# First norm, transposes and value projection in one block by row tiles, and the bias pieces prepared in six parts in the merge stage

## What is computed

```python
xn = rms_norm(h, attn_norm_w[layer])
proj = xn @ w_in[layer]
q_a, k_a, v_a, q_b, k_b, v_b, g_a, g_b = jnp.split(proj, in_split_points(), axis=-1)
...
merged = (jax.nn.sigmoid(g_a) * (y_a @ w_proj_swa[layer])
          + jax.nn.sigmoid(g_b) * (y_b @ w_proj_sb[layer]))
h = h + merged @ w_out[layer]
...
gu = x_blk @ w_gate_up[e] + b_gate_up[e]
u = jnp.clip(gu[:, D_FF:], -SWIGLU_LIMIT, SWIGLU_LIMIT)
act = (u + 1.0) * (g * jax.nn.sigmoid(SWIGLU_ALPHA * g))
return act @ w_down[e] + b_down[e]
```

## Time and profile before

| | |
|---|---|
| median of 3 runs | 2304.51 us (2301.51 to 2306.93) |
| the profiled execution | 2303.3 us, its span 2301.6 us |
| PE busy | 2193.7 us, 95% of the span |
| DVE, ACT, POOL busy | 1595.3, 1325.4, 575.9 us |
| mean granted TensorE clock | 0.979 of full speed |

### The profile page before, as it was taken

One profiled execution on the slowest core, in us unless ns is written; L12 is line 12 of the kernel. 1 busy time (PEld: TensorE's weight loads), 2 busy tenths in 40 slices (PEclk: granted clock), 3 DMA queues, 4 the chain that ended last, 5 costly groups with the idle time before them and its releaser, 6 DMA issues.

```text
span 2301.6 us, 38892 instructions
## 1 busy us (share of the span) xinstructions
PE 2193.7 (95%) x13820; PEld 1693.4 (74%) x13821; DVE 1595.3 (69%) x1572; ACT 1325.4 (58%) x1484; POOL 575.9 (25%) x501
## 2 busy tenths in 40 slices
PE   5999999999979996999999999999999999999997
PEld 5877767677767784777777777787887777777775
DVE  4055767676545335887887887797997778777777
ACT  4156575766444113666666665675776556555665
POOL 3621111111012002132533422232332122212222
PEclk8999999999989997999999999999999999999999
DMA  5011212122165325998998998898998889888883
GB/s 167 24 37 37 81 34 61 32 63 61 53 206 183 125 83 211 385 333 281 346 336 295 345 337 284 304 399 273 402 369 304 289 295 338 277 289 288 306 316 113
DMA packets 266324, 515.66 MB, mean 224 GB/s; under 512 B 33125, under 2 KB 76848, under 8 KB 266156
## 3 DMA queue, kind: packets, MB, share of 16 engines
q1 hardware_dynamic: 239948, 471.38, 57.0%
q0 software_dynamic: 17088, 39.14, 7.2%
q10 hardware_dynamic: 9216, 4.20, 0.6%
HBM read 475.30 MB, written 43.50 MB: 225 GB/s over the span
## 4 chain that ended last, share of the span: by engine, by line
PE 58%; DVE 1%; issue 1%; ACT 1%; DMA 0%; POOL 0%; POOLq 0%; ACTq 0%; DVEq 0%
PE ex_gu L2062 30%; PE ex_yp L2110 15%; PE ex_rest L2084 6%; PE ex_rest L2127 3%; PE ex_gu L2053 1%; PE ex_gu L2020 1%; PE ex_tr L2028 1%; PE ex_gu L2028 1%; PE ex_yp L2099 1%; DVE ex_wlo L1938 0%; PE ex_rest L2078 0%; ACT ex_whi L1682 0%; DMA ex_xg<-xn_s,ex_idx 0%; PE ex_gu L2036 0%; PE ex_tr L2020 0%
## 5 line engine op out<-in xcount | busy, mean ns | idle before, releaser
L1938 DVE TENSOR_TENSOR ex_wlo<-ex_raw,ex_whi 128x2048 fp32r<-128x2048 f32 x387 | 876.6, 2291 | 216.3 <-ACT ex_whi L1682 216.2
L1682 ACT ACTIVATE ex_whi<-ex_raw 128x2048 fp32r<-128x2048 f32 x387 | 735.4, 1925 | 220.8 <-PE ex_gu L2062 151.9
L2062 PE MATMUL ex_gu<-ex_whi,ex_xhi 128*128 128x512 f32 x1024 | 290.3, 405 | 1.0 <-DVE ex_xlo L1979 1.0
L2062 PE MATMUL ex_gu<-ex_whi,ex_xlo 128*128 128x512 f32 x1024 | 275.3, 391 | 0.0
L2062 PE MATMUL ex_gu<-ex_wlo,ex_xhi 128*128 128x512 f32 x1024 | 273.9, 389 | 0.0
L2062 PEld LDWEIGHTS ex_gu<-ex_whi,ex_xhi 128*128 128x128 f32 x1024 | 191.5, 188 | 52.3 <-issue 7.4
L2062 PEld LDWEIGHTS ex_gu<-ex_whi,ex_xlo 128*128 128x128 f32 x1024 | 192.8, 188 | 41.6
L2062 PEld LDWEIGHTS ex_gu<-ex_wlo,ex_xhi 128*128 128x128 f32 x1024 | 192.5, 188 | 40.6
L57 PE MATMUL at_job<-xnT_hi,at_whi 128*128 128x512 f32 x416 | 178.7, 430 | 2.1 <-ACT at_rs L566 2.1
L716 POOL TENSOR_TENSOR at_wlo<-at_raw,at_whi 128x1024 fp32r<-128x1024 f32 x29 | 71.7, 2473 | 427.3 <-ACT at_whi L531 427.3
L59 PE MATMUL at_job<-xnT_hi,at_wlo 128*128 128x512 f32 x416 | 164.5, 395 | 0.0
(11 more groups left out here) (309 smaller groups left out, 3662.1 us busy)
## 6 DMA issues: line engine op xcount, KB each, us to landing
ex_raw<-in_w_gate_up_dram SPq DMA_DIRECT2D x512, 512.0 KB, 7.2
ex_raw<-in_w_down_dram SPq DMA_DIRECT2D x256, 512.0 KB, 6.9
at_raw<-in_w_in_dram SPq DMA_DIRECT2D x25, 512.0 KB
gT<-at_gst SPq DMA_DIRECT2D x32, 256.0 KB, 2.4
mg_g<-gT SPq DMA_DIRECT2D x32, 256.0 KB, 3.0
n_x<-in_x_dram SPq DMA_DIRECT2D x8, 512.0 KB, 8.2
...
```

Source lines behind the costliest of these rows:

```text
L1682: nc.scalar.activation(w_hi[:, i % RING, :], raw[:, i % SLABS, :], ACT.Copy).then_inc(hi_d, 1)
L1938: nc.vector.tensor_tensor(w_lo[:, slot, :], raw[:, i % SLABS, :], w_hi[:, slot, :].bitcast(F32), ALU.subtract).then_inc(lo_d, 1)
L2062: mm = nc.tensor.matmul(gu[:, half, h, :], x[:, k, :], w[:, kk, h, :], start=k == 0 and n == 0, stop=k == KD - 1 and n == 2)
```

## The change

1. The norm and the value projection become one block, `norm_and_values`. PE turns tiles 0 and 1, and then takes in turn the value products of tile t and the transposes of tile t+2. ACT and DVE are written out in the same rhythm: squares and scales three tiles ahead, high and low parts two tiles ahead. The pairs of banks for the products are two instead of four.
2. SP issues the value weights behind row tiles 0 and 1 instead of behind all eight; the other six tiles and attention's first weights follow.
3. The bias pieces are prepared in the merge stage, in six parts of 512 columns (four of gate and up, two of down), with one buffer for the rows and two for the pieces. POOL does a part behind its split for the next tile, in tiles 0 to 5; SP stores a part and loads the next behind the gates of tiles 1 to 6. The loop over tiles on SP and POOL is unrolled for it.

```diff
+def norm_and_values(nc, x, attn_norm_w, w_in, ident, nhalf, raw, raw_in, xnT_hi, xnT_lo, va, vb, x_in):
+
...
+        raw_v = sb("raw_v", [P, KD, VW])
+        w_hi = sb("pv_whi", [P, KD, VW], F32R)
+        w_lo = sb("pv_wlo", [P, KD, VW], F32R)
         tr = ctx.enter_context(nc.psum_tensor("n1_tr", [P, 4, HALF], F32))
-        w_in_ = sem("n1_w_in")
...
             @block.sync
             def _(sp):
-                for t in range(NT):
+                def load_rows(t):
                     sp.dma_start(xin[:, t, :], x_t[t]).then_inc(x_in[t], 16)
-                load_value_weights(sp, w_in, raw_v, rawv_in)
+
+                load_rows(0)
+                sp.dma_start(wB[:, :], attn_norm_w[0:1, :].to_broadcast([P, D])).then_inc(w_in_, 16)
+                load_rows(1)
+                sp.dma_start(raw_v[:, :, 0:P], w_v[:, :, VA:VA + P]).then_inc(rawv_in, 16)
+                sp.dma_start(raw_v[:, :, P:VW], w_v[:, :, VB:VB + HALF]).then_inc(rawv_in, 16)
+                for t in range(2, NT):
+                    load_rows(t)
+                load_first_tiles(sp, w_in, raw, raw_in)
 
             @block.scalar
             def _(act):
-                for t in range(NT):
+                def square(t):
                     act.wait_ge(x_in[t], 16)
-                    if t:
-                        act.wait_ge(sq_done, t)
+                    after(act, sq_done, t)
                     nc.scalar.activation(junk[:, :], xin[:, t, :], ACT.Square,
                                          accum_out=ssq[:, t:t + 1]).then_inc(sq_done, 1)
+
+                def high(t):
+                    for g in range(2):
+                        m = 2 * t + g
+                        act.wait_ge(tr_done, m + 1)
+                        nc.scalar.activation(xnT_hi[:, 4 * g:4 * g + 4, t * P:(t + 1) * P],
+                                             tr[:, m % 4, :].rearrange("p (k c) -> p k c", k=4),
+                                             ACT.Copy).then_inc(hi_done, 1)
+
+                def split_hi(k):
+                    if k == 0:
+                        act.wait_ge(rawv_in, 32)
+                    nc.scalar.activation(w_hi[:, k, :], raw_v[:, k, :], ACT.Copy).then_inc(whi_d, 1)
+
+                def take_first(t):
+                    bank = acc[:, 2 * (t % 2), :]
+                    act.wait_ge(mm_done, 2 * t + 1)
+                    nc.scalar.activation(va[:, t, :], bank[:, 0:P], ACT.Copy)
+                    nc.scalar.activation(vb[:, t, 0:VH - P], bank[:, P:VH], ACT.Copy).then_inc(ev_first, 1)
+
+                square(0)
+                square(1)
+                high(0)
+                high(1)
+                for k in range(KD):
+                    split_hi(k)
+                square(2)
+                for t in range(NT):
+                    if t + 3 < NT:
+                        square(t + 3)
+                    take_first(t)
+                    if t + 2 < NT:
+                        high(t + 2)
 
...
+                def split_lo(k):
+                    dve.wait_ge(whi_d, k + 1)
+                    nc.vector.tensor_tensor(w_lo[:, k, :], raw_v[:, k, :], w_hi[:, k, :].bitcast(F32),
+                                            ALU.subtract).then_inc(wlo_d, 1)
+
+                def take_second(t):
+                    dve.wait_ge(mm_done, 2 * t + 2)
+                    nc.vector.tensor_copy(vb[:, t, VH - P:HALF], acc[:, 2 * (t % 2) + 1, 0:VH]).then_inc(ev_second, 1)
+
+                scale_tile(0)
+                scale_tile(1)
+                low(0)
+                low(1)
+                for k in range(KD):
+                    split_lo(k)
+                scale_tile(2)
+                for t in range(NT):
+                    if t + 3 < NT:
+                        scale_tile(t + 3)
+                    take_second(t)
+                    if t + 2 < NT:
+                        low(t + 2)
+
             @block.tensor
             def _(pe):
...
+                def turn(t):
                     pe.wait_ge(xs_done, t + 1)
+                    for g in range(2):
+                        m = 2 * t + g
+                        after(pe, lo_done, m - 3)
+                        for k in range(4):
+                            last = nc.tensor.transpose(tr[:, m % 4, k * P:(k + 1) * P],
+                                                       xs[:, t % 2, (4 * g + k) * P:(4 * g + k + 1) * P], ident[:, :])
+                        last.then_inc(tr_done, 1)
+
+                def values(t):
+                    pe.wait_ge(lo_done, 2 * t + 2)
                     for h in range(2):
-                        if t >= 4:
-                            pe.wait_ge(ev_second if h else ev_first, t - 3)
+                        if t >= 2:
+                            pe.wait_ge(ev_second if h else ev_first, t - 1)
                         for k in range(KD):
                             if t == 0 and h == 0:
-                                pe.wait_ge(lo_done, k + 1)
-                            last = split3(nc, acc[:, 2 * (t % 4) + h, 0:VH],
+                                pe.wait_ge(wlo_d, k + 1)
+                            last = split3(nc, acc[:, 2 * (t % 2) + h, 0:VH],
                                           xnT_hi[:, k, t * P:(t + 1) * P], xnT_lo[:, k, t * P:(t + 1) * P],
                                           w_hi[:, k, h * VH:(h + 1) * VH], w_lo[:, k, h * VH:(h + 1) * VH],
                                           k == 0, k == KD - 1)
                         last.then_inc(mm_done, 1)
+
+                turn(0)
+                turn(1)
+                for t in range(NT):
+                    values(t)
+                    if t + 2 < NT:
+                        turn(t + 2)
 
 
...
+BIAS_PARTS = 6
+UP_PARTS = (2, 3)
+
+
+def bias_steps(c):
+
+    return 6 + 7 * c + sum(u < c for u in UP_PARTS)
+
+
+def merge(nc, w_proj_swa, w_proj_sb, ident, gT, y_s, mT_hi, mT_lo, w_out, raw_o, raw_o_in, y_in, ring, wo_hi, wo_lo,
+          b_gate_up, b_down, bp_s):
 
...
+        brow = sb("mg_brow", [3 * NE, HALF])
+        pieces = sb("mg_pieces", [P, 2, HALF], BF16)
+        pick = sb("mg_pick", [P, NE], BF16)
+        b_in, b_d, b_out = sem("mg_b_in"), sem("mg_b_d"), sem("mg_b_out")
...
-                over_tiles(sp, body)
+                def load_bias(c):
+                    src = b_gate_up[0, :, c * HALF:(c + 1) * HALF] if c < 4 else b_down[0, :, (c - 4) * HALF:(c - 3) * HALF]
+                    for q in range(3):
+                        sp.dma_start(brow[q * NE:(q + 1) * NE, :], src).then_inc(b_in, 16)
+
+                def store_bias(c):
+                    sp.wait_ge(b_d, bias_steps(c + 1))
+                    sp.dma_start(bp_s[:, c * HALF:(c + 1) * HALF], pieces[:, c % 2, :]).then_inc(b_out, 16)
+
+                load_bias(0)
+                for m in range(KD):
+                    body(m, m % 2, m < KD - 1)
+                    if m in range(1, BIAS_PARTS + 1):
+                        store_bias(m - 1)
+                        if m < BIAS_PARTS:
+                            load_bias(m)
+                sp.dma_start(bp_s[:, 3 * D:3 * D + NE], pick[:, :]).then_inc(b_out, 16)
                 for k in range(4, 4 + EARLY):
                     sp.wait_ge(olo, k - 3)
                     sp.dma_start(raw_o[:, k % 4, :], w_out[0, k * P:(k + 1) * P, :]).then_inc(raw_o_in[k % 4], 16)
+                sp.wait_ge(b_out, 16 * (BIAS_PARTS + 1))
...
+                steps = [0]
+
+                def step(ins):
+
+                    steps[0] += 1
+                    ins.then_inc(b_d, 1)
+                    pool.wait_ge(b_d, steps[0])
+
+                def bias_part(c):
+
+                    pool.wait_ge(b_in, 48 * (c + 1))
+                    if c in UP_PARTS:
+                        step(nc.gpsimd.tensor_scalar(brow[:, :], brow[:, :], 1.0, None, ALU.add))
+                    after(pool, b_out, 16 * (c - 1))
+                    step(nc.gpsimd.tensor_copy(pieces[0:3 * NE, c % 2, :], brow[:, :]))
+                    for first in range(1, 3):
+                        for q in range(first, 3):
+                            mine = slice(q * NE, (q + 1) * NE)
+                            step(nc.gpsimd.tensor_tensor(brow[mine, :], brow[mine, :], pieces[mine, c % 2, :], ALU.subtract))
+                            step(nc.gpsimd.tensor_copy(pieces[mine, c % 2, :], brow[mine, :]))
+
+                for s in range(2):
+                    step(nc.gpsimd.memset(pieces[3 * NE:P, s, :], 0.0))
+                step(nc.gpsimd.memset(pick[:, :], 0.0))
+                for q in range(3):
+                    step(nc.gpsimd.affine_select(out=pick[:, :], in_=pick[:, :], compare_op=ALU.not_equal, fill=1.0,
+                                                 base=-q * NE, pattern=[[-1, NE]], channel_multiplier=1))
                 pool.wait_ge(wlo_d, 3)
-                over_tiles(pool, lambda m, s, more: split_lo(m + 1, 1 - s) if more else None)
+                for m in range(KD - 1):
```

(30 more changed lines are left out.)

93 lines of the change are left out of this document (13 added, 80 removed).

## The result

| | before | after |
|---|---|---|
| median of 4 runs | 2303.04 us (2301.51 to 2306.93) | 2291.18 us (2286.92 to 2295.13) |
| profiled execution, its span | 2303.3, 2301.6 us | 2291.37, 2289.7 us |
| mean granted clock | 0.979 | 0.982 |
| first and last value matmul | 38.55, 96.93 us | 18.27, 81.80 us |

The ratio is 0.9945, 95% interval 0.9929 to 0.9961: faster by 0.55%, 11.9 us. The forecast was 2291 us. The total is right; two of its terms are not, and their errors cancel in part.

A forecast was written before the change was run, and what follows sets the result against it. PE was taken as busy nearly the whole span, so the gain lay in its idle time before the value projection. Terms: -20.4 + 6.5 + 0.7 = -13.2 us, giving 2291 us; range 2287 to 2299 us.

The forecast's parts named there:

- First value matmul: First block: weights issued earlier land at 16.45 us, so PE starts the value projection at 18.1 instead of 38.55: -20.4 us.
- Transposes between projections: First block: six sets of eight transposes now stand between PE's projections at 1.09 us each: +6.5 us, at most 11.8.
- The second rival: First block: PE's clock drops; cold transposes alone give 2296 us (8%), slowed matmuls too give 2308 us (4%).
- The projection: First block: the same 24 matmuls at DVE's pace and 360 at 0.1466 us, nothing just in time: 0.
- Leaving the values stage: Values stage: the bias work moves out, but POOL was done long before PE, so it gains nothing: 0.
- The bias parts in the merge: Merge: POOL's six parts loop through SP in 10.1 us, two in 11.5; the slip stays hidden from PE: 0.
- the forecast's own signs of being wrong: ACT idle on a DMA until 24 us; sets of 1.97 us; PE waiting for mg_wlo or mg_prod in merge tiles 2 to 7.
- the half lock: Merge: DVE holds POOL up by half of 2.8 us a part; loop 11.5 us, slips sum to 3.6 us, inside the slack.
- the slack of 4.4: Merge: a split POOL finishes at 689.16 us is wanted by PE at about 693.6, 4.4 us later.
- the gates wait for DVE's product anyway: Merge: SP's loads go out up to 2.5 us later, gates among them, without harm.
- The rival of the loop: Merge: POOL's short steps cost twice, a part 10.8 us, loop 15.5, 23 us on PE: 2314 us, slower; 5%.
- Start of the merge: Merge start: the first bias load, 192 KB, goes ahead of the first gates and delays PE: +0.7 us, bounds 0 and 1.3.

The follow-up runs named there:

- e3: Changed kernel with the value weights issued behind all eight row tiles; ratio to the kernel before 0.9977.
- before_again: The kernel before, unchanged, run once more for a second trace; ratio to the kernel before 1.0004.
- e2: The changed kernel's merge behind the front of the kernel before (two blocks, without its bias work); ratio to the kernel before 1.0010.
- e1: Changed kernel without bias loads and POOL's bias steps in the merge, stores kept; 2289.66 us, ratio to the kernel before 0.9953.
- after_third: The changed kernel, unchanged, run a third time; ratio to the kernel before 0.9952.
- e4: Changed kernel's single block, but all transposes before all projections, old engine order, value weights behind the row tiles; ratio to the kernel before 1.0015.
- e6: Changed kernel with five POOL steps a bias part instead of seven; ratio to the kernel before 0.9939.
- e8: Changed kernel with two bias-row buffers, five steps a part, and attention's first low half on DVE instead of POOL; 2287.63 us, ratio 0.9937.

## Why the prediction came out right

1. *First value matmul.* Forecast 18.1, measured 18.27: -20.3 for -20.4. The chain was the one described, weights landing at 16.5 (forecast 16.45), and e3 moved them alone and moved the start by 7.8 us, the six row tiles of the earlier trace rows.
2. *Transposes between projections.* Forecast +6.5, measured +5.2 (0.86 a set, not 1.09). The set at 26.10 us in the earlier trace rows was too dear a row: its 1.09 us are a length to the last matmul's modelled end, while in a queue without gaps the next matmul starts 0.79 us after the set's first and is itself 0.08 longer. The second rival did not come true: in the traces of the new order the sets between matmuls ran at full clock, and PE kept it behind them. Nor was its evidence sound. The earlier trace rows has 0.50 from 32 to 36 us, with transposes alone; but with transposes alone the set at 26.10 us took 1.09 us, and in before_again the last three sets did, with a granted clock of 1.00 from 28 to 32 us:

```profile
28.39 1.09 PE L157 MATMUL n_tr<-ident,n_xs 128*128 128x128 f32 x8 [0.42 <-DVE n_xs L136]
```

The Trainium skill (TensorE: Matmul & The Clock Gate, "Part 4: PE-mode transpose") says that a transpose does not count as busy in the same way as a matmul. These sets do not bear it out: PE had done nothing but transposes when its clock rose.

3. *The projection* cost nothing more, as said; tile 2's scaled rows came at 25.3 us (23.98 and 1.31), forecast 25.2.
4. *Leaving the values stage* gave nothing: e2.
5. *The bias parts in the merge.* Forecast 0, measured +2.8. This is the step that failed, and PE waiting for mg_wlo in tiles 2 to 7 was one of the forecast's own signs of being wrong. It did not follow from its own terms. By the half lock that it takes, the two long parts loop in 6.8 + 1.4 + 4.7 = 12.9 us, so the slips sum to 4 x 0.6 + 2 x 2.0 = 6.4 us and not to 3.6, which is 2.0 above the slack of 4.4.

   Nor were the terms right. Its sentence "by columns that is 3 x 1.02 + 4 x 0.46 + gaps = 5.4 us a part" scaled long rows down. Short ones take 1.16 and 0.60 when undisturbed, 6.4 us a part; the 0.14 us of each that don't scale are a quarter of a cast. Beside DVE they take 1.49 and 0.95; over six parts that adds (1365 - 1160) x 18 + (738 - 600) x 18 ns = 6.2 us, 1.0 a part, where 1.4 had been taken by halving the lock. The Trainium skill (SBUF — State Buffer, "Who interferes with whom") states that a DVE operation with two SBUF inputs and a POOL operation that reads SBUF exclude each other. The trace agrees that they hold each other up: both engines paid.

   The way through SP was shorter than forecast, 3.4 us from the end of part 1 (664.52) to the first step of part 2, not 4.7. POOL's split for tile 4 ended at 679.69, 33.2 us behind tile 1's start; in before it was 28.4. Slip 4.8, slack 4.4: the rest is PE's first wait. The 2.8 us are the three waits, 1.75, three times 0.27 that a stop costs beyond its idle time in the starts of the matmuls around it, and 0.2 more before the out-projection. That "the gates wait for DVE's product anyway" did not hold either: DVE stood 12.5 us for ACT's gates in this merge and 2.4 in the one before, though PE did not wait for it.

   The rival of the loop had the mechanism and the threshold (a part of about 7 us decides), and the parts, 7.2 to 9.3 us, lay just above it; at 5% it was rated too low, and its price of 23 us far too high for what happened.
6. *Start of the merge.* Forecast +0.7, measured 0 in the profiled execution: 15.65 us to tile 1 for 15.66. Over all traces with the changed merge it is 15.4 to 18.05, so this one doesn't settle it. In e1, without bias loads, it is 16.92, so these loads are not all of it.

Front -15.1 for -13.9, merge +2.8 for +0.7: -11.9 in the span for -13.2, with 0.4 from the rest. That these 1.3 us do not show in the total is luck: the forecast started from a median of 2304.51 us before, and by the result's four runs that was 2303.04. The rest of the program counts as well: from attention's first matmul to the merge's the traces differ by 5 us. So 2291 was right to a microsecond only with the scatter of runs on its side.

## What to carry over

Ask of a load what is issued ahead of it that isn't needed as early: the order of one queue was 8 us here, at no cost. Before work is cut into small pieces for an engine with "room", price the pieces with rows of small instructions, and write the loop (steps, store, load, landing, the engine's other work) as one period against the consumer's; where it is near, a second buffer or fewer steps each end the waits. Sum the slips over every part, the long ones too. And read a forecast that came true by its terms.

## What had not been expected

- Tile 1 of the merge starts 0.3 to 2.4 us later than before in nine of the twelve traces with the changed merge, e1 without bias loads too: ACT's first sigmoid of the gates came 12.9 to 13.9 us behind the first matmul in seven of them and 14.3 to 15.6 in five, against 13.2 in both traces of before. The first of the gates' loads was issued 6.5 us behind that matmul in e1 and 7.6 in after_third, and the two that this sigmoid needs had landed 8.0 us later in both; 5.4 us later in after. What holds them back is open, and no run of this study tells it.
- The clock's dip behind tile 0 (0.83 to 0.85 as the mean of 10 us) came after waits of 3.10 us and more, in all four traces that have one, and after waits of 1.7 to 2.3 us in three traces of ten, e4, e6 and e8. In those three PE had stood for 0.87 to 1.18 us a few us earlier as well, on mg_yTlo.
- DVE and POOL slow each other in steps: POOL's subtraction on 32x512 takes 1.16 or 1.49 us, its cast 0.60 or 0.95, with hardly anything in between.
